# Sums of squares as a rounded part and a rest: a two-layer encoder step in one kernel

## What is computed

```python
def rms_norm(x, g):
    xf = x.astype(jnp.float32)
    y = xf * lax.rsqrt(jnp.mean(xf * xf, axis=-1, keepdims=True) + NORM_EPS)
    return (y * g.astype(jnp.float32)).astype(x.dtype)

def swiglu(x, w_gate, w_up, w_down):
    a = jnp.einsum('btd,df->btf', x, w_gate)
    b = jnp.einsum('btd,df->btf', x, w_up)
    return jnp.einsum('btf,fd->btd', jax.nn.silu(a) * b, w_down)

def trunk(x, pos, caches, w):
    ...
    for l in range(DEPTH):
        ...
        ff_a = swiglu(rms_norm(x, g[0]), ...)
        x = x + 0.5 * rms_norm(ff_a, g[1])
        h = rms_norm(x, g[2])
        ...
            mix, st = even_mixer(h, pos, i, w, lc)
        ...
            mix, st = odd_mixer(h, pos, i, w, lc)
        ...
        x = x + rms_norm(mix, g[3])
        ff_b = swiglu(rms_norm(x, g[4]), ...)
        x = x + 0.5 * rms_norm(ff_b, g[5])
```

## Time and profile before

| | us |
|---|---|
| median of 3 runs | 2049.3 |
| lowest and highest | 2048.05 and 2049.34 |
| the profiled execution, its own time | 2048.42 |
| its span, first to last instruction | 2046.6 |
| PE busy | 2030.3 (99%) |
| DVE, ACT, POOL busy | 981.9, 749.6, 123.9 |

### The profile page before, as it was taken

The page is one execution under the profiler, slowest core; times in us unless marked ns, Lnnn a source line. Parts: engine busy times, 40 slices in busy tenths (PEclk is TensorE's granted clock), DMA queues, the critical chain, the costliest instruction groups (busy, mean ns, idle before and its releaser), DMA issues.

```text
span 2046.6 us, 40704 instructions
## 1 busy us (share of the span) xinstructions
PE 2030.3 (99%) x16824; PEld 1980.0 (97%) x16824; DVE 981.9 (48%) x1593; ACT 749.6 (37%) x1462; POOL 123.9 (6%) x158
## 2 busy tenths in 40 slices
PE   9999999999999999999999999999999999999997
PEld 9999999999669999999999999999997999999997
DVE  7444431474674754443137444431566574444213
ACT  6323322332675433232234323231438542223221
POOL 0000000000101000000000000000125200000000
PEclk9999999999999999999999999999999999999999
DMA  4322232232311222222322222222240222222312
GB/s 151 100 85 82 83 101 97 70 101 78 111 43 43 83 86 98 82 82 88 110 63 91 82 86 98 90 95 76 91 135 25 78 74 91 94 82 90 114 57 72
DMA packets 49468, 176.85 MB, mean 86 GB/s; under 512 B 6016, under 2 KB 10448, under 8 KB 49248
## 3 DMA queue, kind: packets, MB, share of 16 engines
q1 hardware_dynamic: 47216, 167.66, 25.0%
q0 software_dynamic: 2160, 7.87, 1.2%
HBM read 168.33 MB, written 5.36 MB: 85 GB/s over the span
## 4 chain that ended last, share of the span: by engine, by line
PE 98%; DVE 1%; ACT 0%; DMA 0%; issue 0%; DVEq 0%; SPq 0%
PE psum L603 30%; PE psum L604 30%; PE psum L602 30%; PE psum L866 1%; PE psum L767 1%; PE psum L852 1%; PE psum L988 1%; PE psum L811 1%; PE psum L971 1%; PE psum L943 0%; PE psum L829 0%; PE psum L720 0%; PE psum L715 0%; DMA x<-in_x 0%; ACT probsC L1263 0%
## 5 line engine op out<-in xcount | busy, mean ns | idle before, releaser
L602 PE MATMUL psum<-xhi,w_hi 128*128 128x272 f32 x3360 | 972.2, 289 | 1.5 <-DVE xlo L1625 1.5
L603 PE MATMUL psum<-xlo,w_hi 128*128 128x272 f32 x3360 | 968.3, 288 | 0.0
L604 PE MATMUL psum<-xhi,w_lo 128*128 128x272 f32 x3360 | 965.7, 287 | 0.0
L602 PEld LDWEIGHTS psum<-xhi,w_hi 128*128 128x128 f32 x3360 | 633.3, 188 | 4.1 <-DVE w_lo L475 2.2
L603 PEld LDWEIGHTS psum<-xlo,w_hi 128*128 128x128 f32 x3360 | 632.9, 188 | 0.5
L604 PEld LDWEIGHTS psum<-xhi,w_lo 128*128 128x128 f32 x3360 | 631.8, 188 | 0.0
L499 DVE TENSOR_TENSOR w_lo<-w_raw,w_hi 128x1024 fp32r<-128x1024 f32 (+2 forms) x276 | 351.5, 1309 | 375.9 <-ACT w_hi L490 375.7
L604 PE MATMUL psum<-h_hi,w_lo 128*128 128x272 f32 x1408 | 407.0, 289 | 0.0
L602 PE MATMUL psum<-h_hi,w_hi 128*128 128x272 f32 x1408 | 406.6, 289 | 0.0
L603 PE MATMUL psum<-h_lo,w_hi 128*128 128x272 f32 x1408 | 404.7, 287 | 0.0
L490 ACT ACTIVATE w_hi<-w_raw 128x1024 fp32r<-128x1024 f32 (+2 forms) x276 | 296.8, 1118 | 94.5 <-PE psum L604 78.4
(11 more groups left out here) (236 smaller groups left out, 1367.5 us busy)
## 6 DMA issues: line engine op xcount, KB each, us to landing
w_raw<-in_w_gate_up SPq DMA_DIRECT2D x172, 512.0 KB, 3.6
w_raw<-in_w_down SPq DMA_DIRECT2D x64, 704.0 KB, 4.2
w_raw<-in_even_in SPq DMA_DIRECT2D x16, 512.0 KB, 4.1
w_raw<-in_odd_in SPq DMA_DIRECT2D x10, 512.0 KB, 4.1
w_raw<-in_even_out SPq DMA_DIRECT2D x8, 512.0 KB, 3.6
w_raw<-in_odd_out SPq DMA_DIRECT2D x8, 512.0 KB, 4.9
out_band_kv<-qkvb POOLq DMA_DIRECT2D x1, 2176.0 KB, 10.8
out_y<-x SPq DMA_DIRECT2D x8, 272.0 KB, 2.6
```

The costliest lines, as they stand in the source:

```text
L602: nc.tensor.matmul(out, s_hi, m_hi, start=first, stop=False)
L603: nc.tensor.matmul(out, s_hi, m_lo, start=False, stop=False)
L604: return nc.tensor.matmul(out, s_lo, m_hi, start=False, stop=last)
```

## The change

Four things are changed at once.

1. **Totals in two parts.** POOL, once it has the last sum of a half, rounds the total into a float32r tile (total_hi) and subtracts (total_lo). post_sum waits for total_low and multiplies both with ones, now of type float32r. For half 0 of every sub-layer, POOL sums all eight tiles (whole_total), and post_last of half 0 goes. In an FFN the products of half 0 move from step 4 to step 12 of (6,1); in a mixer from step 4 of (0,1) to step 3 of (1,1), and ACT takes the result (0,1) ahead of the root. For half 1, post_sum keeps its place and post_last stays a float32 product. The products with ones ahead of a sub-layer and for the latents stay float32.
2. **The start.** WARM is 12 and each of these products has 136 columns in place of 272; the second weight group is loaded and split in two halves of columns; ones comes through a raw tile, which ACT rounds; DVE puts rests between the sums of squares.
3. **Sliding-window attention.** Scores of items 2 and 3 move into the last input projection, to steps 1 and 5 of its second unit; turn(0) follows right behind it. The corner is filled ahead of the shuffles. DVE's reciprocal of item 1 comes one turn later, and the last projection's read-out with the steps of its rotation moves one or two items later.
4. **Counting.** The events of sum_y are counted by tables (summed_tiles, total_base), since halves have 8 and 7 tiles.

```diff
-WARM = 4
+WARM = 12
...
+def whole_total(s, H):
+
+    return H == 0
...
+                    if (m, H) == [tile for tile in summed_tiles(s) if tile[1] == H][-1]:
+                        hi, lo = split_total(s, H)
+                        pool.wait_ge(ysq_summed, total_event(s, m, H) + 1)
+                        nc.gpsimd.tensor_copy(hi, total).then_inc(total_high, 1)
+                        pool.wait_ge(total_high, 2 * s + H + 1)
+                        nc.gpsimd.tensor_tensor(lo, total, hi.bitcast(F32), ALU.subtract).then_inc(total_low, 1)
...
             def post_sum(s, H):
 
-                pe.wait_ge(ysq_summed, total_event(s, KD - 2, H) + 1)
-                nc.tensor.matmul(psum[:, 6 + H, 0:TH], ones[:], total_of(s)[:, HALF[H]], start=True, stop=False)
+                whole = whole_total(s, H)
+                hi, lo = split_total(s, H)
+                pe.wait_ge(total_low, 2 * s + H + 1)
+                nc.tensor.matmul(psum[:, 6 + H, 0:TH], ones[:], hi, start=True, stop=False)
+                mm = nc.tensor.matmul(psum[:, 6 + H, 0:TH], ones[:], lo, start=False, stop=whole)
+                if whole:
+                    mm.then_inc(poststat, 1)
...
             def post_first_half(s):
                 post_sum(s, 0)
-                post_last(s, 0)
+                if not whole_total(s, 0):
+                    post_last(s, 0)
...
                     if last and n == 2:
-                        mid, at = (lambda: post_first_half(s)), 4
+                        mid, at = (lambda: post_first_half(s)), 12
                     elif last and n == 3:
                         mid, at = (lambda: post_sum(s, 1)), KF // 2
...
-                    if n == KD:
-                        mixer_half(s, m, H, range(KD), lambda: post_first_half(s), 4)
+                    if n == KD + 1:
+                        mixer_half(s, m, H, range(KD), lambda: post_first_half(s), 3)
...
                     s = c - 1
+                    if SUBS[s] != "ffn":
+                        mixer_result(s, 0, 1)
                     post_std(c, 0)
...
-                nc.tensor.matmul(psum[:, 7, 0:TH], rstd[:, 0:P], rstd[:, 0:TH], start=True, stop=True)
+                nc.tensor.matmul(psum[:, 7, 0:TQ], rstd[:, 0:P], rstd[:, 0:TQ], start=True, stop=True)
...
-                                        mids={(0, 3): lambda: swa_scores(s, 0), (0, 6): lambda: swa_scores(s, 1)})
+                                        mids={(0, 3): lambda: swa_scores(s, 0), (0, 6): lambda: swa_scores(s, 1),
+                                              (1, 1): lambda: swa_scores(s, 2), (1, 5): lambda: swa_scores(s, 3)})
...
-                for n in range(2, N_SWA):
+                turn(0)
+                for n in range(4, N_SWA):
                     swa_scores(s, n)
-                    if n >= 3:
-                        turn(n - 3)
-                    if n >= 4:
-                        values(n - 4)
+                    turn(n - 3)
+                    values(n - 4)
```

More of the change, by code:

```diff
@@ L418, in total_of, with split_total @@
             return total_ffn if SUBS[s] == "ffn" else total_mix
+        def split_total(s, H):
+            i = 0 if SUBS[s] == "ffn" else 1
+            return total_hi[i][:, HALF[H]], total_lo[i][:, HALF[H]]
         def pre_gain(c):
@@ L488, in act_split @@
                 hi, _ = weights(g, par, u)
-                cols = slice(D // 2 if isinstance(g, int) and g == 0 else 0, n)
+                cols = slice(split_from(g), n)
                 nc.scalar.activation(hi[:, cols], raw_of(g, u)[:, cols], ACT.Copy).then_inc(w_hi_done, 1)
@@ L612, in in_half @@
                 opening = c == 0 and H == 0
+                second = isinstance(g, int) and g == 1 and H == 0
                 if opening:
@@ L622, in in_half @@
                         pe.wait_ge(w_lo_done if k else first_lo, u + 1)
+                    elif second and k in (0, 4):
+                        pe.wait_ge(w_lo_done if k else first_lo, 2 * g + u + 1)
                     elif k == 0 and not tilewise:
@@ L648, in pre_total @@
                     cols = slice(TH + part * TQ, TH + (part + 1) * TQ)
-                    mm = nc.tensor.matmul(psum[:, 2 + part, SPARE], ones[:], total_x[:, cols], start=True, stop=True)
+                    mm = nc.tensor.matmul(psum[:, 2 + part, SPARE], ones[:].bitcast(F32), total_x[:, cols], start=True, stop=True)
                 mm.then_inc(prestat, 1)
@@ L1336, in boundary @@
                             high_part(c, 0, k)
-                    split_group(act, "act", 1)
+                    for u in range(2):
+                        first_split(act, "act", 1, u)
+                        split_unit(act, "act", 1, u)
                     for k in range(KD):
                         square(c, 0, k)
+                    act.wait_ge(ones_in, 16)
+                    nc.scalar.activation(ones[:], ones_raw[:], ACT.Copy).then_inc(ones_rounded, 1)
                     act.wait_ge(x_in[4], 16)
@@ L1957, in sum_y @@
                 for m, H in out_order(SUBS[s]):
[L1958 removed]
+                    if (m, H) not in summed_tiles(s):
                         continue
```

96 lines of the change are left out of this document (58 added, 38 removed).

## The result

| | before | after |
|---|---|---|
| median | 2049.2 us (2048.1 to 2049.5, 6 runs) | 2062.0 us (2060.1 to 2063.2, 6 runs) |
| profiled execution | 2048.4 us | 2060.1 us, span 2058.3 |
| mean granted clock over the span | 0.998 | 0.996 |

The change makes the kernel slower by 0.64%: the ratio is 1.0064, with a 95% interval of 1.0055 to 1.0074. The forecast was 2050.6 us and the range ended at 2056.3, so both missed, on the low side.

The account below looks back on a forecast made before the run. PE, busy 99% of the span at the higher clock, was taken as the bound. Products -5.3, FFN waits +9.9, start -1.0 and attention -1.8 summed to +1.8 us; forecast 2050.6 us, range 2047.0 to 2056.3.

Parts of the forecast that it names:

- The size of POOL's two instructions: FFN ends, half 1: rounding 0.5 us and difference 1.0 us on POOL, within a PE wait of 3.3 us.
- Rounding at over 1 us: Sign against the forecast: POOL's rounding of a total taking more than 1 us.
- The rival: Clock falls in the three new FFN-end waits: 1.7 us lost each, +5.1, in all +6.9 us, 2056.2 us; chance 0.13.
- So the wait is not given back: Ends of three FFNs: later work moves 2.35 us too or waits for PE anyway, so +9.9 us stays.
- Products with ones: All six sub-layers: float32r products at 0.125 us save PE 0.88 us each, -5.3 us in all.
- Mixers and last FFN: No new PE wait: POOL needs 1.5 us more against 2.5 of room (last FFN), ending 1.3 ahead in a mixer.
- Start: Kernel start: clock up earlier, but inputs then bind, the last rests of x; -1.0 us, bounds -1.2 and +0.5.
- Attention: Sliding-window attention: waits of 1.5 us for exponentials and 0.3 us for the corner go; -1.8 us, bounds -2.2 and -1.0.
- first copy on ACT that now waits for turn(0): Sliding-window attention: named as part of the price of moving scores into the projection, with no separate size.

Follow-up runs that it names:

- the filled wait: Changed kernel plus 36 unread products of ones and h_hi ahead of the total_hi product in (7,1), sub-layers 0, 2, 3: 2055.7 us, ratio 1.0034.
- result (6,1) first: Changed kernel, but at an FFN's end ACT takes result (6,1) and its squares right behind half 0's root, ahead of four x tiles: 2049.7 us, ratio 1.0003.
- sum later: Changed kernel with only half 1's sum later in the FFNs, at step 21 of (7,1) for 11: 2048.6 us, ratio 0.9999.
- seven tiles and a late sum: Changed kernel, but in FFNs half 0 totals seven tiles at old step 4 and half 1's sum is at step 16 of (7,1): 2043.2 us, ratio 0.9973.

## Why the prediction was wrong

Most of the chain held to a few hundredths. Shifted by the start's 0.87 us, the forecast put the root at 394.73, the end of the squares of (6,1) at 402.86, POOL's sum at an end of 404.0 and PE's arrival at 402.39. The trace has 394.72, 402.85, 403.99 and 402.41. Two steps failed.

- **The size of POOL's two instructions** ("I take 0.5 for the rounding, nearest the copy ... and 1.0 for the difference, since DVE splits weights meanwhile"). They took 1.29 and 1.61, 1.40 us more, both above the upper bounds (1.06 each). The wait, from PE's arrival to the product, is 4.7 us for 3.3, three times +1.4: +4.1 us. Two errors are in it. DVE's work was counted for the difference and not for the rounding; and the bounds were taken from a sum (1.06) that ran beside DVE's rests of 272 columns, 0.49 us each, where the new pair runs beside two instructions of 1024 columns, 1.24 and 1.42 us. The runs have the series: 0.41 and 0.77 beside nothing (and again with the wide ones taken away), 0.68 and 0.85 or 0.61 and 1.02 beside 272 columns, 0.79 and 1.13 beside 544, 1.29 and 1.61 beside 1024. "Rounding at over 1 us" stood among the signs that would show the forecast wrong.
- **The clock was made an alternative with a chance of 0.13.** It came on top: 1.4, 1.6 and 1.6 us in the profiled execution, 2.0 to 2.1 us at each place in the medians, by the filled wait. The rival priced it at 1.7, which was about right; what was wrong was to treat a wait of twice the longest known gap as more likely harmless than not, when no row showed any gap of that length. The slices of the earlier trace rows, 51 us each, could not have shown it either: three falls left every one of them at 9. The Trainium skill, TensorE: Matmul & The Clock Gate, section "HAM oscillation — how this bites in real kernels", says that the half clock comes back after an idle gap, and the trace agrees: 0.66 to 0.76 granted in the stretches behind the 4.5 us waits. The gap that the section names as too long is longer than the 1.77, 2.79 and 3.04 us behind which the clock also fell in the experiments; there the measurement decides. With the sizes of this trace the rival gives 1.8 + 4.1 + 4.7 = 10.6 us, and 12.2 with the 2.1 of the medians.
- **"So the wait is not given back"** was right: the ends cost 4.7 + 1.4 - 0.9 = 5.2 us once and 4.7 + 1.6 - 0.9 = 5.4 twice, and 5.3, 5.5 and 5.5 were found. The reason given, that the rests of x and PE are late alike, was also a warning not followed to its end: when the first wait is taken away (result (6,1) first; sum later), the squares of (7,1) turn up as a wait in their own right. The rests of x never did at these three places.
- **Products with ones**: -5.3 us forecast. The places where nothing else moved (sub-layers 1, 4 and 5) show -0.85, -0.85 and -0.84 for 0.88 each. The kernel with seven tiles and a late sum confirms the price in time: 3.4 us below the one without split totals, 2 x 0.88 + 4 x 0.42 = 3.4 by the forecast's terms.
- **Mixers and last FFN**: no wait, as forecast, though with less room. In sub-layer 1 POOL's pair took 1.35 and 1.13, so the parts stood at 680.03, and PE's product with total_hi is at 680.82: 0.8 us of room for 1.3.
- **Start**: -0.87 for -1.0. The clock is up from 7.26 on, and then the inputs bind, one wait of 0.26 us at 11.28 among them, for a rest of weights rather than of x. The part varies from execution to execution, with waits of PE for rests of x or of weights (0.3 to 0.9 us) at other places of the start: POOL's copy of half 1, at 300.01 before and at 299.14 after, stands between 298.63 and 300.01 in the profiled executions of the experiments, so against the one trace of before it was worth from 0 to 1.4 us. That -1.0 came out so nearly is in part luck.
- **Attention**: -1.1 for -1.8. The 1.5 and 0.3 us are gone. One wait for turned probabilities is new, 0.24 us at 1558.56, the "first copy on ACT that now waits for turn(0)"; the other 0.2 us of that line (1592.91) stood in the kernel before too (1579.52). It was named as a price and not taken into the value. The rest is in no row of waits but in the starts: scores of items 2 and 3 together took 1.4 us of PE behind the projection (1540.83 to 1542.40, less one ordinary step), and 0.9 and 1.0 us inside it (1552.62 to 1553.78 and 1555.02 to 1556.28, less two steps each). So they cost 0.5 us more where they stand among ordinary matmuls, which the forecast put at nothing.

The sum by terms, on the profiled executions: forecast +1.8, found +11.7, 9.9 apart. The longer waits are 4.1 of it, the clock 4.7, the attention 0.7, start and products 0.1 each: 9.7 us. The 0.2 left are in no row that was read.

One reading of the rows was short of what they hold: apart from the start, "the longest" waits of PE were given as 1.5 and 0.3 us. The same view has one of 0.5 us (squares at the end of the last FFN, 2035.51) and one of 0.4 us in the even mixer. Both stand in the changed kernel as well, so the sum is not touched.

Open remains what decides whether the clock falls behind a gap, and for how long; the runs only show how often it did (below).

## What to carry to other kernels

Where one engine is busy for 99% of the time, a product saved is worth its duration, and an event moved later is worth whatever hangs on it: before moving 24 matmuls ahead of a statistic, write down everything that its consumer's engine does afterwards in order, and ask of each item when it is needed, not of the first alone. Price a new instruction on GpSimd beside what VectorE runs at that very time, by when the VectorE instruction under way there ends; the wide ones are the dear ones. And count a new wait of TensorE as its length plus a spell at the lower clock as soon as it is longer than the gaps that the trace shows to be harmless; often the cheapest mend is to ask later (here step 16 for 11), and not to work faster.

## What was not expected of the hardware

- **The same gap, two outcomes.** In the kernel with result (6,1) first all three gaps are 1.77 us long; behind the first the clock stayed at the upper level, behind the others it fell (granted clock by stretch):

```profile
405.00:410.00 5.00, 3.23 (x27) 3.02 (x25) 4.68 (x8) 3.51 (x10) 3.01 (x7) 1.00 0.50 162
...
1080.00:1085.00 5.00, 5.00 (x35) 5.00 (x34) 4.97 (x5) 1.53 (x2) 0.00 (x0) 0.81 0.10 8
1480.00:1485.00 5.00, 3.96 (x17) 3.75 (x18) 4.70 (x6) 2.42 (x5) 0.95 (x2) 0.66 0.72 248
```

Over all runs, at the ends of sub-layers 0, 2 and 3: behind gaps of 0.7 to 0.8 us (six places) and of 1.5 us (nine places) it never fell; behind 1.8 us at two of three, 2.8 at three of three, 3.0 at two of three, 4.5 to 4.6 at all six. These are counts from one to three traces at each length, and no run tells what decides between the two outcomes.

- **It can fall behind the gap.** In the changed kernel PE starts again at 1484.40 at the upper level, 0.29 us a matmul, and only from 1485.13 on are the matmuls longer:

```profile
1484.40 0.39 PE L754 MATMUL psum<-total_hi,ones 128*128 128x272 f32 x1 [4.52 <-POOL total_lo L2028]
...
1485.01 0.29 PE L637 MATMUL psum<-h_hi,w_lo 128*128 128x272 f32 x1
1485.13 0.39 PE L635 MATMUL psum<-h_hi,w_hi 128*128 128x272 f32 x1
1485.32 0.43 PE L636 MATMUL psum<-h_lo,w_hi 128*128 128x272 f32 x1
```

- **VectorE and GpSimd stretch each other.** Beside POOL's pair the two 128x1024 differences took 2.58 us, and 2.36 with nothing on POOL. In the kernel without them one of 64 columns took 0.24 us between POOL's sum (to 403.49) and its rounding (from 403.55), and 0.60 beside POOL's difference.

```profile
403.33 0.24 DVE L532 TENSOR_TENSOR w_lo<-w_raw,w_hi 128x64 fp32r<-128x64 f32 x1 [0.47 <-ACT w_hi L521]
404.28 0.60 DVE L532 TENSOR_TENSOR w_lo<-w_raw,w_hi 128x64 fp32r<-128x64 f32 x1 [0.71 <-ACT w_hi L521]
```
